# Modulation's weight slabs on four column groups of TensorE, with a new order at the first long convolution and cross-attention products in parts

## The reference, cut to what matters

```python
mod_x = silu_c @ w_mod + b_mod            # 1024 x 6144, one row
mod_c = silu_cc @ w_mod + b_mod           # same weights, context's row
hx = modulate(rmsnorm(x, norm_mix), sh_a, sc_a)
...
w = softmax(q0 @ k0) - lam * softmax(q1 @ k1)     # 4 heads, 512 x 768
attn = rmsnorm(w @ v, subln) * (1 - lam_init)
...
for n, gate in enumerate((x1, x2)):               # as products of spectra
    z = gate * (long_conv(z, k_f[:, n]) + hy_skip[n] * z)
x = x + g_a * (concat(attn, rmsnorm(z, hy_norm)) @ w_out)
...
x = x + softmax(rmsnorm(x) @ w_q @ k.T / 16) @ v @ w_o   # cross attention, 4 heads
```

## Time and profile before

| | |
|---|---|
| median of 3 runs | 1778.08 us (1777.21 to 1779.16) |
| the profiled execution | 1775.0 us |
| its span in the trace | 1773.2 us |
| mean granted clock of TensorE | 0.990 |
| TensorE busy | 1701.6 us (96%) |
| VectorE busy | 978.9 us (55%) |
| ScalarE busy | 694.0 us (39%) |
| GpSimd busy | 141.8 us (8%) |

### The profile page before, as it was taken

One profiled execution on the slowest core, in us unless ns is written; L12 is line 12 of the kernel. 1 busy time (PEld: TensorE's weight loads), 2 busy tenths in 40 slices (PEclk: granted clock), 3 DMA queues, 4 the chain that ended last, 5 costly groups with the idle time before them and its releaser, 6 DMA issues.

```text
span 1773.2 us, 18754 instructions
## 1 busy us (share of the span) xinstructions
PE 1701.6 (96%) x7182; PEld 1282.2 (72%) x7182; DVE 978.9 (55%) x1344; ACT 694.0 (39%) x1040; POOL 141.8 (8%) x150
## 2 busy tenths in 40 slices
PE   7999998989999999999999999999998999999997
PEld 1478765356778888888788877558875788888886
DVE  5867576356464423445679688565534453535362
ACT  2632354311344322335564656955533331213131
POOL 0312000014200000003000000213000100000001
PEclk9999999989999999999999999999999999999999
DMA  9334122411232232223242121424311132222221
GB/s 319 121 119 150 65 60 98 154 69 35 68 89 95 84 107 95 95 77 108 93 160 84 48 60 37 159 78 164 132 59 48 48 139 98 96 95 95 95 95 48
DMA packets 113239, 174.48 MB, mean 98 GB/s; under 512 B 3787, under 2 KB 56523, under 8 KB 112716
## 3 DMA queue, kind: packets, MB, share of 16 engines
q1 hardware_dynamic: 109404, 160.76, 26.7%
q0 software_dynamic: 3760, 12.72, 2.2%
HBM read 169.00 MB, written 4.46 MB: 98 GB/s over the span
## 4 chain that ended last, share of the span: by engine, by line
PE 82%; DVE 8%; ACT 5%; issue 2%; DMA 2%; POOL 1%; SPq 0%; DVEq 0%; ACTq 0%; POOLq 0%
PE bank L848 15%; PE bank L850 15%; PE bank L849 15%; PE bank L881 6%; PE bank L882 6%; PE bank L886 5%; PE bank L906 3%; PE bank L1092 2%; PE bank L955 2%; PE bank L1105 1%; PE bank L1035 1%; PE bank L1047 1%; PE bank L1235 1%; PE bank L1387 1%; PE bank L1418 1%
## 5 line engine op out<-in xcount | busy, mean ns | idle before, releaser
L3051 POOL TENSOR_TENSOR arena<-arena 128x512 f32<-128x512 f32 (+1 forms) x56 | 77.2, 1385 | 968.0 <-ACT arena L1519 964.3
L850 PE MATMUL bank<-hx_hi,weight_slots_lo 128*128 128x512 f32 x320 | 125.3, 391 | 0.0
L1488 ACT ACTIVATE weights_hi<-weight_slots 128x2048 fp32r<-128x2048 f32 (+2 forms) x46 | 77.0, 1725 | 110.6 <-DMA weight_slots<-in_ffn_w_down 57.7
L3006 DVE TENSOR_TENSOR weight_slots_lo<-weight_slots,weights_hi 128x2048 fp32r<-128x2048 f32 x30 | 67.4, 2289 | 95.4 <-ACT weights_hi L2173 95.4
L2173 ACT ACTIVATE weights_hi<-weight_slots 128x2048 fp32r<-128x2048 f32 x30 | 55.8, 1908 | 161.2 <-DMA weight_slots<-in_w_up 116.8
L849 PE MATMUL bank<-xn_lo,weights_hi 128*128 128x512 f32 x288 | 112.1, 389 | 0.0
L1474 ACT ACTIVATE arena<-bank 128x512 f32<-128x512 f32 (+3 forms) x110 | 54.8, 537 | 137.7 <-PE bank L850 50.5
L848 PE MATMUL bank<-sq_hi,weights_hi 128*128 128x512 f32 x256 | 99.6, 389 | 0.0
L849 PE MATMUL bank<-sq_lo,weights_hi 128*128 128x512 f32 x256 | 99.6, 389 | 0.0
L850 PE MATMUL bank<-sq_hi,weight_slots_lo 128*128 128x512 f32 x256 | 99.6, 389 | 0.0
L2214 DVE TENSOR_TENSOR weight_slots_lo<-weight_slots,weights_hi 128x2048 fp32r<-128x2048 f32 (+2 forms) x36 | 70.2, 1991 | 29.3 <-ACT weights_hi L1488 29.3
(11 more groups left out here) (423 smaller groups left out, 4138.6 us busy)
## 6 DMA issues: line engine op xcount, KB each, us to landing
weight_slots<-in_w_in SPq DMA_DIRECT2D x24, 1024.0 KB, 7.2
weight_slots<-in_ffn_w_up SPq DMA_DIRECT2D x22, 1024.0 KB, 6.6
weight_slots<-in_w_up SPq DMA_DIRECT2D x16, 1024.0 KB, 6.4
weight_slots<-in_w_down SPq DMA_DIRECT2D x16, 1024.0 KB, 6.2
weight_slots<-in_w_mod SPq DMA_DIRECT2D x14, 1024.0 KB, 8.2
arena<-in_w_mod POOLq DMA_DIRECT2D x32, 256.0 KB, 3.3
weight_slots<-in_w_out SPq DMA_DIRECT2D x8, 1024.0 KB, 7.7
weight_slots<-in_w_xkv SPq DMA_DIRECT2D x8, 1024.0 KB, 7.4
```

What stands on the lines that cost most here:

```text
L850: return mm(ps, ll, rh, start=False, stop=stop)
L1488: A(high_half(kind, n, i), W[:, s_, a:b], ACT.Copy).then_inc(w_hi, 1)
L3006: V.tensor_tensor(W_lo[:, s % 2, a:b], W[:, s % 2, a:b], W_hi[:, s % 2, a:b].bitcast(F32), ALU.subtract).then_inc(w_lo, 1)
L3051: G.tensor_tensor(acc, acc, sq[i % 2][:, 0:width], ALU.add).then_inc(sq_added, 1)
```

## The change

1. **Four column groups.** `silu_c` is widened to 32 columns per k tile (30 of them zero) and cleared by VectorE at the start. The 8 matmuls of a slab go to column groups k % 4 of the array and so to rows 0, 32, 64 and 96 of the bank (two matmuls added in each). ScalarE copies all 128 rows, and `modulation_columns` multiplies them by `pick` (128x2, ones in the rows of each group's two lines), which turns lines to columns and adds the groups.
2. **Order at the convolution.** The last head's output, its norm and slab 11's columns move behind the transposes of the first order (norm sum after the first pair of Z); VectorE folds right after the last transposes of attention. `zt` and `obuf` get other tiles.
3. **`lows=4` in out's `first_products`.** Behind the norm sum at k = 4, the low products of k tiles 0 to 3 are made.
4. **Cross attention.** Two of the late query products are cut in two halves; out3's first four tiles are made in two parts: k tiles 0 to 3 as finished banks `out3a_m` in steps 11, 12, 14 and 15, added to the residual by VectorE, and k tiles 4 to 7 as before.

```diff
-O_STEPS = {6: 0, 10: 1, 14: 2, 17: 3}
-NORM_O_STEPS = {7: 0, 11: 1, 15: 2, 18: 3}
+O_STEPS = {6: 0, 10: 1, 14: 2}
+NORM_O_STEPS = {7: 0, 11: 1, 15: 2}
-XQ_STEPS = [3, 5, 8, 10]
+XQ_STEPS = [3, 4, 7, 10]
+XQ_PARTS = {2: (0, 0, 4), 3: (0, 4, 8), 4: (1, 0, 8), 6: (2, 0, 4), 7: (2, 4, 8), 10: (3, 0, 8)}
+XO_FIRST = [11, 12, 14, 15]
...
     for o in range(2):
         j += [f"zt_{o}_{t}" for t in range(NT)]
+        if o == 0:
+            j += [f"o_{HEADS - 1}", "modc_11"]
         for m in range(HC):
             j += [f"Zre_{o}_{m}", f"Zim_{o}_{m}"]
+            if (o, m) == (0, 0):
+                j += [f"norm_o_{HEADS - 1}"]
...
-        silu = sb("silu_c", [P, KD, 2])
+        silu = sb("silu_c", [P, KD, 32])
+        pick = sb("pick_rows", [P, 2])
-        zt = tiles(56, 4)
+        zt = tiles(0, 4)
-        obuf = tile(14)
+        obuf = tile(83)
...
                 for k in range(KD):
                     if k == at:
                         middle()
+                        for k_ in range(lows):
+                            ready_lo(k_)
+                            for m, ps in enumerate(banks):
+                                mm(ps[:, 0:width], wh(k_, m), x2[1][:, k_, 0:width], start=False, stop=False)
                     ready_hi(k)
...
-                    for k in range(KD):
+                    for k in range(lows, KD):
                         ready_lo(k)
...
                 for k in range(KD):
-                    ins = mm(ps[0:2, :], silu[:, k, :], w[:, k, :], start=k == 0, stop=k == KD - 1)
+
+                    g = 32 * (k % 4)
+                    ins = mm(ps[g:g + 32, :], silu[:, k, :], w[:, k, :], start=k < 4, stop=k >= KD - 4, tile_position=(0, g))
                 end(ins)
...
-                        ins = nc.tensor.transpose(ps[:, 2 * m:2 * m + 2], mod_row[s % 2][0:2, P * m:P * m + P], ident[0:2, 0:2])
+                        ins = mm(ps[:, 2 * m:2 * m + 2], mod_row[s % 2][:, P * m:P * m + P], pick[:], start=True, stop=True)
...
-            first_products("out", "mix", (mix_hi, mix_lo), middle=lambda: norm_sum("norm_hy"), at=4)
+            first_products("out", "mix", (mix_hi, mix_lo), middle=lambda: norm_sum("norm_hy"), at=4, lows=4)
...
-                    k = 3 * (n - XH * NT)
-                    out3_high(range(k, k + 3))
+                    out3_high([KD // 2 + n - XH * NT])
...
+                if n in XO_FIRST:
+                    m = XO_FIRST.index(n)
+                    w = split_slab("xo", 0)
+                    ps = begin(f"out3a_{m}")
+                    c = slice(P * m, P * m + P)
+                    for k in range(KD // 2):
+                        operand("ao", k)
+                        ins = mm3(ps[:], w[0][:, k, c], w[1][:, k, c], ao_hi[:, k, :], ao_lo[:, k, :], k == 0, k == KD // 2 - 1)
+                    end(ins)
...
-                copy(mod_row[s % 2][0:2, :], f"mod_{s}", PS[jobs[f"mod_{s}"] % 8][0:2, :])
+                copy(mod_row[s % 2], f"mod_{s}", PS[jobs[f"mod_{s}"] % 8][:])
...
+            V.memset(silu[:], 0.0).then_inc(sem("silu_zero"), 1)
             for n in range(3):
                 sine_argument(n)
+                if n == 0:
+                    loaded(dve, "con")
+                    V.tensor_reduce(pick[:], ident.rearrange("p (j r) -> p r j", r=32)[:, 0:2, :], AX, ALU.add).then_inc(sem("pick_ready"), 1)
...
-            for s in (9, 10, 11):
-                mod_column(s)
-            head_norm(HEADS - 1)
+            mod_column(9)
...
-            dve.wait_ge(normed, sum(norms[f"norm_o_{HEADS - 1}"]))
+            done(dve, f"wt_{HEADS - 1}_{NT - 1}_1")
             for c in range(HC):
                 fold(0, c)
+            for s in (10, 11):
+                mod_column(s)
...
+                    if (o, m) == (0, 1):
+                        head_norm(HEADS - 1)
...
+                if n in XO_FIRST:
+                    residual("out3a", [XO_FIRST.index(n)])
```

More of the change, by code:

```diff
@@ L133, in job_plan @@
     j += ["modc_6", "hy_0", "hy_1", "modc_7"]
-    for n in range(HEADS * NT + 3):
+    for n in range(HEADS * NT + 2):
         if n < HEADS * NT:
@@ L871, in split_product, with together @@
                 end(ins)
-            def together(banks, wh, wl, x2, ready_hi, ready_lo, done_one, middle=None, at=KD, width=L):
+            def together(banks, wh, wl, x2, ready_hi, ready_lo, done_one, middle=None, at=KD, width=L, lows=0):
                 for k in range(KD):
@@ L892, in first_products @@
                 together([open_bank(f"{kind}_{m}") for m in range(4)], hi, lo, x2,
-                         lambda k: pe.wait_ge(x_hi, operand_no[op, k] + 1), lambda k: operand(op, k), end, middle, at, width)
+                         lambda k: pe.wait_ge(x_hi, operand_no[op, k] + 1), lambda k: operand(op, k), end, middle, at, width, lows)
             def modulation(s):
@@ L1083, in _ @@
                             end(ins)
+                if o == 0:
+                    head_output(HEADS - 1)
+                    modulation_columns(11)
                 loaded(pe, "dft_z")
@@ L1386, in out3_high @@
                         for part in w:
-                            mm(ps[:], part[:, k, P * m:P * m + P], ao_hi[:, k, :], start=k == 0 and part is w[0], stop=False)
+                            mm(ps[:], part[:, k, P * m:P * m + P], ao_hi[:, k, :], start=k == KD // 2 and part is w[0], stop=False)
             for n in range(XH * NT + 2):
                 if n >= XH * NT:
-                    k = 3 * (n - XH * NT)
-                    out3_high(range(k, k + 3))
+                    out3_high([KD // 2 + n - XH * NT])
                 if n < XH * NT:
@@ L1422, in _ @@
             for m, ps in enumerate(out3_banks):
-                for k in range(KD):
+                for k in range(KD // 2, KD):
                     operand("ao", k)
@@ L1664, in attention_exp, with output_copied, output_norm @@
                               psum_free[jobs[name] % 8], 1)
+            def output_copied(h):
+                if h:
+                    act.wait_ge(normed, norms[f"norm_o_{h - 1}"][0] + 1)
+                copy(obuf, f"o_{h}", PS[jobs[f"o_{h}"] % 8][:])
+            def output_norm(h):
+                evicted(act, f"o_{h}")
+                norm_stat(f"norm_o_{h}", lambda k: obuf, features=2 * DH)
             def split_hyena(n, m):
@@ L1688, in _ @@
                 if n in O_STEPS:
-                    h = O_STEPS[n]
-                    if h:
-                        act.wait_ge(normed, norms[f"norm_o_{h - 1}"][0] + 1)
-                    copy(obuf, f"o_{h}", PS[jobs[f"o_{h}"] % 8][:])
+                    output_copied(O_STEPS[n])
                 if n in NORM_O_STEPS:
-                    h = NORM_O_STEPS[n]
-                    evicted(act, f"o_{h}")
-                    norm_stat(f"norm_o_{h}", lambda k: obuf, features=2 * DH)
+                    output_norm(NORM_O_STEPS[n])
             for o in range(2):
@@ L2980, in low_mlp @@
                                            ALU.mult, ALU.subtract).then_inc(x_lo, 1)
+            for m in range(4):
+                evicted(dve, f"out3a_{m}")
             residual("out3", [0, 1, 2, 3, 4])
```

31 lines of the change are left out of this document (20 added, 11 removed).

## The result

| | before | after |
|---|---|---|
| median | 1778.26 us | 1753.49 us (1750.88 to 1759.20, 4 runs) |
| profiled execution | 1775.0 us | 1750.88 us |
| span | 1773.2 us | 1749.1 us |
| mean granted clock | 0.990 | 0.981 |

The ratio is 0.9872, 95% interval 0.9858 to 0.9887: 1.3% faster, with 1752 forecast. The two profiled executions lie 24.1 us apart, against 25.9 in the prediction's sum, but several terms came out otherwise than forecast. I read the new trace in the prediction's order. Outputs of TensorE have the names of the job plan: h for the filter network's layers, mod and modc for a slab and its columns, Z for the products with the transform, o and out for the two output products.

What follows compares the result with a forecast made beforehand. TensorE, busy 96% of the span, was taken as the bound. Terms 3.5 + 21.5 + 0.6 + 0.3 = 25.9 us off 1775.0 gave 1749.1, with the median's 3.1 more 1752; 8 in 10 for 1744 to 1764.

Steps and rivals of the forecast that it cites:

- Slabs on four groups, 1.9 to 2.1 us: Modulation slabs at start and in attention: four column groups run at once, 5 us less than 7.03 per slab.
- Start, 3.5 us: Filter network and first spectra: shorter slabs let h3 start earlier, gaining 3.5 us of a possible 20 (bounds 2.5 and 5.8).
- from there VectorE sets the pace: Start, from h3 on: VectorE's filters run without a gap, 28.7 to 41.1; second order 4.4 us earlier.
- End of attention 13: Last heads of attention: shorter slabs mod_8 to mod_11 bring modc_10 from 354.24 to 339.5, up to 342.5 at half clock.
- new order 8.5: First convolution: early folding and transposes bring Z 7.1 us nearer, and Z itself takes 1.5 less at full clock.
- Output projection, 0.6: First output projection: low products fill the norm's wait, gaining 0.6 us of 3.0; a 2.5 us wait remains before out_4.
- Cross attention, 0.3: Cross attention: waits covered and newly bare give 1.5 us, clock may cost 1.7; 0.3 taken, bounds -1.4 and +1.5.
- Clock rival: Three new gaps (52 to 59, 327 to 331, 1333 to 1339) each bring 10.3 us half clock, not 3.4: 1762; chance 0.15.
- Half clock over 5 us after a new gap: After any new TensorE gap: half clock lasting over 5 us was a sign that the forecast is wrong.
- No concurrency: Modulation slabs: groups do not overlap and slabs stay at 7.03 us, total 1773; chance 0.12.
- the slower case: Modulation slabs: groups queue and each record shows its weight load, 1.4 us more per slab, total 1784; chance 0.03.
- Two groups: Modulation slabs: only two groups run at a time, 3.6 us per slab, total 1756.5; chance 0.17.

Runs made afterwards that it cites:

- e5: Changed kernel with a slab's 8 matmuls on two column groups instead of four: 1751.94 us, ratio 0.9869.
- the first trace: Profiled execution of the changed kernel, 1750.88 us; the second is the same kernel without an edit, profiled once more, 1760.48 us.
- e10: Changed kernel with 3 overwritten full-array products put in front of each of the start's slabs mod_0 and mod_1: 1749.67 us, ratio 0.9847.
- e8: Changed kernel with slabs 0 to 3 made serially as before, only slabs 8 to 11 on four groups: 1752.64 us, ratio 0.9866.
- e1: Kernel before with part 1 alone (four column groups, no new order): 1766.38 us, ratio 0.9951.
- e2: Changed kernel without part 1, slabs serial on two columns again, the rest kept: 1765.27 us, ratio 0.9945.
- e7: Changed kernel with VectorE forming the low half of out's second slab before out_0's residual instead of behind it: 1754.73 us, ratio 0.9871.
- e3: Changed kernel with part 4 undone, so with before's cross attention: 1756.41 us, ratio 0.9877.
- e6: Changed kernel with narrow overwritten products filling three of TensorE's waits at the start: 1764.28 us, ratio 0.9915.

## Why the prediction was right, and where it wasn't

- **Slabs on four groups, 1.9 to 2.1 us: right** (1.92), and columns + 0.65 (1.05 for 0.40) too. The nearest row, the scores on halves, was the right guide; e5 shows the law between. The Trainium skill, "TensorE: Matmul & The Clock Gate", section "Packing small matmuls", lets a load overlap running matmuls only for another row group; here four groups share their rows and no such cost shows: a slab is over 7.03/1.92 = 3.7 times as fast.
- **Start, 3.5 us: wrong**, 0.2 in the first trace, and a loss of 6.5 in the second (norm_x's sum at 72.89 for 66.33). The step that failed is "from there VectorE sets the pace", which took full clock up to 52 for granted. TensorE fell to half at 27, set the pace of the second order, and the gap before modc_3 shrank to 1.9 us. e10, with the clock full over h4_0, gives the forecast's course, shifted: h3 at 20.29 for 19.0, ScalarE's copy of mod_3's lines at 60.02 for 59.1, and the spectra on again behind norm_x at 65.93, for 64.2 forecast with half clock there and 68.15 before. e8 shows that the whole term is worth nothing as built. The prediction looked for half clock only behind long gaps; the earlier trace rows shows it there, but nothing there excludes it elsewhere.
- **End of attention 13, new order 8.5: right**, with 21.5 for both. From the spectra behind norm_x to the second Z the first trace gained 22.8, the second 21.3; e1 and e2 have 14.8 and 9.8 for the parts. In the first trace 1.5 of it were given back at once, where after had half clock for 6.8 us in the second Z, for 3.4 before.
- **Output projection, 0.6: right** (0.5 at out_4, wait 2.62 for 2.5). e7 shows the cause, and that behind it a second wait of the same size was hidden: the possible 3.0 needed two more edits, not one.
- **Cross attention, 0.3: the size is off, -2.1.** The wait of 3 us was found in its place (2.82), and 1.56 before xo_0 for the 1.3, and the 1.0 of part 4 at equal clock lies in the bounds. The term's clock cost was mis-sized: the prediction had 1.7 as a chance only. In before's own cross attention 6.8 us of half clock cost 2.8 to 3.1 us (e1, e3 against before), so it isn't part 4's either.
- **Clock rival.** Of the three named gaps none had 10.3 us of half clock: the one at 327 had 3.4, the start's didn't arise, the third 6.8. As a mechanism it was nonetheless closest to what took the start's gain. "Half clock over 5 us after a new gap" was named as what would make the forecast wrong, and it happened. That the time came within 1.5 us of the forecast is luck: 4.8 us came back in the second block, which no term has; without them it would be some 1758.
- **Other rivals.** No concurrency and the slower case fell with the first slab's row. Two groups were given 1756.5; built, they came to 1751.94, no worse than four, so the price set on the longer slab was high by what the clock's stretches alone can move. The no-concurrency rival gave the order and the rest 7.6 us with slow slabs; e2, which is that kernel with the old columns, gained 9.6.

So the sum's 25.9 and the measured 24.1 agree partly by offset: -3.2 (start, 0.25 for 3.5), +1.3 (attention and order), -1.5 (clock in the second Z), -2.4 (cross attention), +4.8 (second block), and -0.8 for the rest.

## What to carry to other kernels

Column groups side by side cut the time of narrow fp32 products almost by their number (3.7 times for four), but here the shorter slabs at the start went with a fall of TensorE's clock that cost as much as they saved: check the granted clock behind the place, and judge by several executions. Products whose result is thrown away may keep the clock up; here six of the full array, overwritten afterwards, made up in one trace for the 8.0 us that they took and left 2.2 against before. When a wait is removed, read whose queue (here ScalarE's, standing for a slab's landing in front of ready work) is next, and change both together.

## What the runs showed of the hardware that was not expected

- TensorE stayed at half clock for up to 37.5 us without an idle gap in its records (e6), where the same h4 products ran at full clock behind full-array products (e10) or behind slabs of 7.03 us on two columns (before, e2, e8). e6 and e10 start these products at the same time (26.89 and 26.88). The runs exclude idle time as the only cause, and show that the work in front matters; which property of it counts is not settled.
- The same kernel held that half clock for 17.1 us in one execution and 37.5 in another; the two executions of before agreed in place and length of every such stretch ahead of the last 10 us.
- Half clock of 3.4 or 6.8 us in the cross attention and near 1150 came and went with edits far away from there, and between two executions of the changed kernel, worth up to 4.8 us: a gain of that size in a stage that an edit doesn't touch is no evidence.
